# A transformer block on one core: three modulation groups (9, 16 and 17) are loaded and accumulated earlier

## What is computed

```python
mods_x = split((silu(c) @ w_mod + b_mod), 6)      # w_mod is 2048 x 12288
sa, sca, ga, sf, scf, gf = mods_x
nx = rmsnorm(x, g) * (1 + sca) + sa
q_a, kv_a, k_rope, g_b, g_c, hh = split(nx @ w_in)
o_conv = g_b * conv3(g_c * hh)
o_mla = softmax attention (8 heads; queries and keys from q_a, kv_a, k_rope, low rank)
h = x + ga * (concat(rmsnorm(o_mla), rmsnorm(o_conv)) @ w_out)
h = h + gf * moe(modulated(h, sf, scf))           # 32 experts, top 4, and a shared expert
out = rmsnorm(h)
```

## Time and profile before

| | before |
|---|---|
| median of 3 runs | 1110.08 us |
| lowest and highest | 1109.07 and 1110.60 us |
| profiled execution | 1106.52 us |
| its span | 1104.6 us |
| TensorE matmul busy | 1010.1 us, 91% of the span |
| VectorE busy | 551.4 us, 50% |
| ScalarE busy | 223.2 us, 20% |
| bytes moved | 380.34 MB, mean 344 GB/s |

### The profile page before, as it was taken

How to read it: one execution, slowest core, us unless ns; L and a number is a source line. 1 busy time by engine, 2 the same in 40 slices (tenths; PEclk the granted TensorE clock), 3 DMA queues, 4 the chain that set the end, 5 groups by cost and what they waited for, 6 DMA issues and landing times.

```text
span 1104.6 us, 15716 instructions
## 1 busy us (share of the span) xinstructions
PE 1010.1 (91%) x6042; PEld 565.5 (51%) x6043; DVE 551.4 (50%) x1094; ACT 223.2 (20%) x451; POOL 23.9 (2%) x33
## 2 busy tenths in 40 slices
PE   3999998999999889999999999988899898998975
PEld 2644487888885345444485645433343333433421
DVE  3100359754824694985582335544346334544523
ACT  5311120000002363010241212221112203213212
POOL 1000010000002001000000000000000000000002
PEclk9999998999999999999999999999899998999998
DMA  9999998999855747999739999999999999999994
GB/s 356 391 390 388 350 358 264 371 354 327 284 182 172 255 144 261 387 387 334 235 108 383 399 409 408 409 408 407 409 409 407 408 407 409 409 407 409 409 405 166
DMA packets 158362, 380.34 MB, mean 344 GB/s; under 512 B 10498, under 2 KB 44112, under 8 KB 157136
## 3 DMA queue, kind: packets, MB, share of 16 engines
q1 hardware_dynamic: 158288, 379.35, 91.6%
HBM read 377.22 MB, written 2.10 MB: 343 GB/s over the span
## 4 chain that ended last, share of the span: by engine, by line
PE 65%; DMA 13%; SPq 9%; DVE 9%; issue 3%; ACT 1%; POOL 0%; DVEq 0%; POOLq 0%; ACTq 0%
PE ps L674 64%; DMA ring<-in_w_exp_down 8%; SPq L547 4%; DVE part L1664 4%; SPq L542 3%; DMA ring<-in_w_mod 3%; DMA qkv<-in_w_mod 1%; DVE tiny L1851 1%; DVE xres L2136 1%; SPq L553 1%; DMA ring<-in_w_exp_up 1%; DVE kq L1614 0%; PE ps L748 0%; ACT nreg L1477 0%; DVE nreg L1614 0%
## 5 line engine op out<-in xcount | busy, mean ns | idle before, releaser
L674 PE MATMUL ps<-nreg,ring 128*128 128x256 f32 (+2 forms) x1312 | 307.7, 398 | 4.2 <-DVE ring L1856 4.1
L674 PEld LDWEIGHTS ps<-nreg,ring 128*128 128x128 f32 (+1 forms) x1312 | 243.7, 190 | 63.5 <-issue 30.6
L1664 DVE SCALAR_TENSOR_TENSOR part<-ring,csT,part 128x512 f32<-128x512 f32 x232 | 174.7, 753 | 9.2 <-DMA ring<-in_w_mod 0.3
L674 PE MATMUL ps<-ring,nreg 128*32 128x512 f32 (+1 forms) x1344 | 173.4, 599 | 3.4 <-DMA ring<-in_w_exp_up 3.0
L674 PE MATMUL ps<-ring,conv 128*32 128x512 f32 (+2 forms) x688 | 103.5, 656 | 23.7 <-DMA ring<-in_w_exp_down 22.9
L674 PE MATMUL ps<-ring 128*128 128x512 f32 x256 | 110.7, 592 | 0.0
L674 PEld LDWEIGHTS ps<-ring,nreg 128*32 128x32 f32 (+1 forms) x1344 | 48.6, 114 | 111.0 <-issue 110.9
L2136 DVE TENSOR_TENSOR xres<-xres,ps 128x512 f32<-128x512 f32 x96 | 61.6, 683 | 48.5 <-PE ps L674 48.5
L674 PEld LDWEIGHTS ps<-ring 128*128 128x128 f32 x256 | 48.6, 190 | 60.4 <-issue 60.0
L674 PEld LDWEIGHTS ps<-ring,conv 128*32 128x32 f32 (+2 forms) x688 | 29.5, 125 | 89.2 <-issue 85.5
L674 PE MATMUL ps<-nreg,conv 128*128 128x512 bf16 x228 | 57.9, 379 | 11.8 <-DVE xres L2136 8.7
(11 more groups left out here) (285 smaller groups left out, 864.5 us busy)
## 6 DMA issues: line engine op xcount, KB each, us to landing
ring<-in_w_mod SPq DMA_DIRECT2D x78, 1024.0 KB, 11.1
ring<-in_w_exp_gate SPq DMA_DIRECT2D x128, 512.0 KB, 13.6
ring<-in_w_exp_up SPq DMA_DIRECT2D x128, 512.0 KB, 15.2
ring<-in_w_exp_down SPq DMA_DIRECT2D x128, 512.0 KB, 14.5
ring<-in_w_in SPq DMA_DIRECT2D x12, 2048.0 KB, 13.0
ring<-in_w_out SPq DMA_DIRECT2D x8, 2048.0 KB, 11.7
ring<-in_w_mod SPq DMA_DIRECT2D x3, 2048.0 KB, 18.0
ring<-in_w_in SPq DMA_DIRECT2D x3, 1664.0 KB, 16.2
```

The source lines that it names most:

```text
L674: return nc.tensor.matmul(o, l, r, start=start, stop=stop)
L1664: ins = V.scalar_tensor_tensor(out=out_, in0=w_, scalar=scale, in1=acc_, op0=ALU.mult, op1=ALU.add)
```

## The change

Three parts.

1. SyncE issues group 9's four quarters ahead of conv(0,2)'s weights, no longer behind them, and VectorE accumulates group 9 ahead of the statistics, no longer behind them.
2. Group 16 is loaded into `mslot`, each quarter when group 15 leaves it, behind the query weights in SyncE's order. VectorE accumulates its first quarter ahead of projection tile 1 and the others behind the copies of tiles 1, 3 and 7. ScalarE waits for the end of that before it writes the first keys (tile 12). Group 17 takes group 16's old place: into `aslot` when the queries are done and group 16 is accumulated, and accumulated behind the copies of tiles 17, 19, 21 and 23.
3. Attention keeps only group 18: 16 steps, four in each of the iterations 1 to 4. Group 17's sum is taken in iteration 1, no longer 4.

```diff
-        ACC_STEPS = (5, 5, 5, 5, 4, 4, 4, 0)
-        SUM_IN = {4: 17, 7: 18}
+        ACC_STEPS = (0, 4, 4, 4, 4, 0, 0, 0)
+        SUM_IN = {1: 17, 7: 18}
...
             load_conv(0, 1, CONV0 + 2 * CW)
+            load_group(9, 13, mslot, freed_by_dve)
             load_conv(0, 2, CONV0)
-            load_group(9, 13, mslot, freed_by_dve)
...
                 sp.dma_start(slot[s][:, 0:3072].rearrange("p (k n) -> p k n", k=4), wq[:, :, 768 * s:768 * s + 768])\
                   .then_inc(w_full[s], 16)
+            load_group(16, 8, mslot, freed_by_dve)
             sp.wait_ge(conv_full, 24)
...
             sp.wait_ge(proj_full, 12)
-            load_group(16, 8, aslot)
-            load_group(17, 9, aslot, freed_by_dve)
+            sp.wait_ge(acc_done, 16 * (16 - 8) + 16)
+            load_group(17, 9, aslot)
...
                 elif j < 20:
+                    if j == 12:
+                        sc.wait_ge(acc_done, 16 * (ATT_GROUP - 8) + 16)
                     dst, src = knT[:, j - 12, :], bank
...
             kv_gain(0)
             kv_gain(1)
+            accumulate(9, 1, by_feature=True)
             ve.wait_ge(stat_full, 1)
...
-            accumulate(9, 1, by_feature=True)
             conv_rows(0)
             conv_products(0)
...
+            accumulate(ATT_GROUP, 0, mslot, (0,))
             for j in range(1, 28, 2):
...
+                if j in (1, 3, 7):
+                    accumulate(ATT_GROUP, 0, mslot, ({1: 1, 3: 2, 7: 3}[j],))
                 if j in (17, 19, 21, 23):
-                    accumulate(ATT_GROUP, 0, aslot, ((j - 17) // 2,))
+                    accumulate(ATT_GROUP + 1, 1, aslot, ((j - 17) // 2,))
...
             def accumulate_steps(first, count):
                 for i in range(first, first + count):
-                    accumulate(ATT_GROUP + 1 + i // 16, (i // 16 + 1) % 2, aslot, (i % 16 // 4,), (i % 4,))
+                    accumulate(ATT_GROUP + 2, 0, aslot, (i // 4,), (i % 4,))
```

## The result

Over four runs each the changed kernel took 1099.66 us (1098.02 to 1101.24) and the kernel before 1110.34 (1109.07 to 1111.47): a ratio of 0.9905, with a 95% interval from 0.9886 to 0.9924. Five more runs on another chip gave 1100.62 against 1108.62, 0.9922 (0.9909 to 0.9935). Between the two profiled executions the difference is 8.5 us (1106.52 and 1098.02), and that one can be followed from stage to stage.

The account below looks back on a forecast made before the run. TensorE bounds the stages before the experts, expert loads bound theirs, so earlier gains pass through. Group 9's 5.5 plus attention's 2.8 make 8.3 us: 1110.08 to 1101.8 us; 8 in 10 runs from 1098.2 to 1105.4.

Parts of the forecast that it names:

- hole of 7.5 us: TensorE around 180 to 190 us, ahead of group 9's sum: 4.9 us stall plus 0.9 and 1.7 at half speed.
- the half clock: Behind the old stall, TensorE at 1.2 GHz from 185.02 to about 190.2 us: losses of 0.9 and 1.7 us.
- Landing in the order of issue: Convolution loads: with group 9 issued first, its quarters land at 148.4 to 157.5 us, conv(0,2) at 163.5.
- The rival by which the swap does nothing: Group 9's loads: transfers share DMA engines, last quarter still at 163.5, stall 7.5 us; 1109.9 in all. Chance 4%.
- The new stall: TensorE ahead of conv(0,2), waiting for the gate copies until 168.0: 2.0 us, bounds 1.3 and 4.4.
- the rival: Ahead of conv(0,2): a stall of some 3.6 us brings the clock down, losing 2.6 us; 1106.0 in all. Chance 10%.
- the slow spacing: Group 9's quarters land 3.9 us apart, the last at 160.3; as a bound this gives a 4.4 us stall.
- Net gain of part 1: Group 9's move in the convolution: 7.5 us won less a 2.0 us stall, 5.5 us net.
- Group 16 under the queries: Its load and accumulation during the query projections cost 0; between -0.3 and +2 us if a quarter is late.
- attention, 2.8 forecast: Fewer VectorE steps in attention shorten TensorE's waits on head copies: 2.17 + 0.6 us, bounds 0 and 4.1.
- The second copy: Copy of head 2 in attention's iteration 4: about 0.7 us late where it was 1.3, a gain of 0.6.
- All after attention unchanged: Loads of group 18 and the output cost 0; the expert stage stays as long as before, 537 us.

Follow-up runs that it names:

- the split: Changed kernel with group 9's last quarter accumulated behind the statistics: 1096.02 against 1108.62 us for the kernel before, 0.9891; again 1095.85 against 1110.10, 0.9885.
- the filler in the kernel before: Kernel before with five identity products in TensorE's 4.9 us stall ahead of group 9's sum: first stage 315.66 us, 2.5 less than before.
- the reciprocal in its old place: Ahead of iteration 1's maxima; one run moved this convolution-norm reciprocal behind them, in the changed kernel with group 9's last quarter behind the statistics: 1094.33 us, 0.9868.

## Why the prediction was right, and where it was not

The time fell as forecast and within the range: 1101.8 forecast, 1099.66 measured; 8.3 us forecast, 8.5 between the profiled executions. Both parts worked by the mechanism that was forecast. That the sum agrees to 0.2 us is luck: two of its terms were off by 1.3 us each, with opposite signs.

- **The hole of 7.5 us** was right: 7.62 with the split, of which the half clock is 2.5 (forecast 2.6) by the filler in the kernel before.
- **Landing in the order of issue** was right to 0.3 us. The quarters were at 148.1 to 157.6 (forecast 148.4 to 157.5), conv(0,2) at 163.6 (163.5). The run with the old order shows that the forecast stood on this. The rival by which the swap does nothing was wrong in its premise. What it said would follow from quarters that come late is what that run shows, only larger: a stall of 8.7 us and not 7.5.
- **The new stall** was right: 2.0 forecast, 1.7 measured.
- **Wrong: the clock behind it.** The sum had nothing for it; it took 1.7 us. "In attention 2.17 us of standing left it at 1.00" was one observation, and I read it as a bound, gave the rival 10% and let it begin at 3.6 us (and said "as with the slow spacing", for which the bounds above it give 4.4). The clock fell behind this stall in four of the five profiles that have it (1.72, 1.56, 1.48 and 1.64 us; not behind 1.67), and in attention behind the same 2.17 us in two of three. Net gain of part 1: 4.15 and not 5.5. The Trainium skill (TensorE: Matmul & The Clock Gate, What's actually happening) says that the moment of the change of clock varies from run to run. The traces agree: in the two profiles of the changed kernel the fall came at 169.3 and at 168.2.
- **Group 16 under the queries, 0**: right; 52.69 and 52.68 us, TensorE's only listed wait there being the 0.9 at its end that was there before.
- **Mis-sized: attention, 2.8 forecast, 4.07 measured.** 2.17 us went as said. The second copy was late by 0.43 and not 0.7, so the listed waits fell by 3.1. The other 1.0 us no row lists as idle; TensorE's busy time in attention fell too, from 49.50 to 48.62 us. Of that 1.0 us 0.7 stands in iteration 2, around the copy of head 0. The eight transposes there show a part of it. TensorE's timeline of the kernel before:

```profile
390.07 1.27 PE L980 MATMUL ps<-cst,nreg 128*128 128x128 f32 x8
```

  and of the changed one:

```profile
386.63 1.04 PE L981 MATMUL ps<-cst,nreg 128*128 128x128 f32 x8
```

  From the start of the values ahead of them to the end of these transposes it is 3.25 us before (388.09 to 391.34) and 2.77 after (384.90 to 387.67). And where TensorE doesn't stand, its next row starts 0.17 us ahead of that end (387.50), so a stall costs more than the idle time that is listed for it. Another 0.24 us stands in iteration 4, where no wait is listed. Why the transposes took longer is not shown.
- **All after attention unchanged**: right, 676.48 and 676.21 us to the end.
- **The range.** Its lower end, 1098.2, doesn't follow from the terms given: 1098.5 less 0.8 is 1097.7. The measured time lies above both.
- **The spread of the runs.** The old attention is 57.25 us long in one profile and 58.94 and 58.95 in two, when the clock falls behind its 2.17 us stall. With the new steps it is 53.17 to 53.22 in all nine profiles that have them and the reciprocal in its old place. So where the clock falls in attention, the change gains 1.7 us more than the two profiled executions of the comparison show; how often it falls in unprofiled runs was not measured. Why the experts' stage takes 2.5 us more in some executions of one and the same kernel is open too.

## What to carry to other kernels

Where work is moved into an idle stretch, follow the work behind it up to the engine that sets the end, and cut the moved piece to fit the hole: three quarters of group 9 gave 7.6 us, all four only 4.15. A load's place in the issuing queue belongs to the move; here it decided its sign. Ask of a new stall of TensorE what the clock does behind it, even where it is only one or two microseconds: ahead of conv(0,2) it doubled the price in four of five profiles. One trace in which it doesn't fall is no bound.

## What the runs showed of the hardware

Over the 14 profiles TensorE stands 29 times for 1.48 to 2.22 us ahead of the experts' stage, and the granted clock fell to 0.50 behind 8 of these: four of five ahead of conv(0,2), two of three in attention, but one of eight at 27 us (behind 2.22 us, with group 17's sum in iteration 4) and one of thirteen at 73 us (behind 1.65, in the second profile of the split). So the length of a stall alone doesn't decide it; what does is not shown. Behind stalls of 1.46 us and less it did not fall there. In the six cases ahead of conv(0,2) and in attention the fall cost about 1.7 us. The two at the start, where TensorE waits for weights, cost nothing that the first stage shows.

It may fall after the work has begun again: in the changed kernel at about 169.3, with TensorE at work since 167.87. Products with the identity in the stall kept it at 1.00 in all three runs that had them.

Transfers from SyncE landed in the order of issue in the two orders that were run: with group 9 issued first its quarters were there at 148.1 to 157.6 us and conv(0,2)'s weights at 163.6; with the weights first, the first quarter was there only at 154.0.
